# Hybrid DeltaNet and forgetting-attention layer on one core: TensorE multiplies with the values before it computes the scores of a slot

## What is computed

```python
log_f = jax.nn.log_sigmoid(f_logit + f_bias)
cum = jnp.cumsum(jnp.moveaxis(log_f, 2, 1), axis=-1)
for i in range(s // Q_BLOCK):
    lo, hi = i * Q_BLOCK, (i + 1) * Q_BLOCK
    logits = (jnp.einsum('bhqd,bhkd->bhqk', q[:, :, lo:hi], k[:, :, :hi]) * scale
              + cum[:, :, lo:hi, None] - cum[:, :, None, :hi])
    logits = jnp.where(s_pos[None, :] <= t_pos[:, None], logits, -jnp.inf)
    p = jax.nn.softmax(logits, axis=-1)
    outs.append(jnp.einsum('bhqk,bhkd->bhqd', p, v[:, :, :hi]))
```

## Time and profile before

| | us |
|---|---|
| median of 3 runs | 1672.39 |
| lowest, highest run | 1666.14, 1672.8 |
| the profiled execution, its own time | 1669.44 |
| its span, first to last instruction | 1667.3 |
| TensorE busy (matmul) | 1561.4 |
| VectorE, ScalarE, GpSimd busy | 921.2, 692.0, 626.6 |

### The profile page before, as it was taken

One profiled execution on the slowest core, in us unless ns is written; L12 is line 12 of the kernel. 1 busy time (PEld: TensorE's weight loads), 2 busy tenths in 40 slices (PEclk: granted clock), 3 DMA queues, 4 the chain that ended last, 5 costly groups with the idle time before them and its releaser, 6 DMA issues. The chain is left out here.

```text
span 1667.3 us, 22226 instructions
## 1 busy us (share of the span) xinstructions
PE 1561.4 (94%) x7916; PEld 1232.5 (74%) x7916; DVE 921.2 (55%) x1427; ACT 692.0 (42%) x1307; POOL 626.6 (38%) x547
## 2 busy tenths in 40 slices
PE   7999999999999999999749999999999999959998
PEld 5888888888878888888626776766676777637886
DVE  7355545555277668001136676666677766434765
ACT  0346363636211111311005766766676776720100
POOL 1212121202211111110115887867787887901111
PEclk9999999999999999999859999999999999979999
DMA  6134343434753333224491646553555542162642
GB/s 243 46 122 139 89 146 95 135 102 126 115 124 124 122 114 106 68 74 107 124 234 30 166 114 168 140 140 89 140 144 158 154 110 80 38 219 89 202 139 88
DMA packets 191009, 206.81 MB, mean 124 GB/s; under 512 B 50836, under 2 KB 134548, under 8 KB 187860
## 3 DMA queue, kind: packets, MB, share of 16 engines
q1 hardware_dynamic: 189588, 200.35, 42.9%
q10 hardware_dynamic: 1312, 5.05, 0.8%
HBM read 129.98 MB, written 75.30 MB: 123 GB/s over the span
## 5 line engine op out<-in xcount | busy, mean ns | idle before, releaser
L1437 POOL TENSOR_TENSOR m_p_lo<-m_p,m_p_hi 128x512 fp32r<-128x512 f32 (+1 forms) x320 | 373.6, 1189 | 85.8 <-ACT m_p_hi L1394 82.2
L507 PE MATMUL bank<-x_hi,w_hi 128*128 128x512 f32 x992 | 394.5, 398 | 4.1 <-DVEq L801 4.1
L507 PE MATMUL bank<-x_hi,w_lo 128*128 128x512 f32 x992 | 387.8, 391 | 0.0
L507 PE MATMUL bank<-x_lo,w_hi 128*128 128x512 f32 x992 | 387.2, 390 | 0.0
L532 POOL TENSOR_TENSOR w_lo<-w_raw,w_hi 128x512 fp32r<-128x512 f32 x66 | 97.6, 1500 | 498.0 <-ACT w_hi L588 498.0
L1392 ACT ACTIVATE m_p<-m_st,m_fcol 128x512 f32<-128x512 f32 (+1 forms) x320 | 204.1, 638 | 186.3 <-PE m_st L1268 93.1
L1500 DVE TENSOR_REDUCE m_maxima<-m_aux 128x1 f32<-128x512 f32 (+2 forms) x320 | 195.3, 619 | 140.3 <-PE m_aux L1238 90.3
L507 PEld LDWEIGHTS bank<-x_hi,w_hi 128*128 128x128 f32 x992 | 186.8, 188 | 40.9 <-issue 4.5
L507 PEld LDWEIGHTS bank<-x_hi,w_lo 128*128 128x128 f32 x992 | 186.6, 188 | 39.8
L507 PEld LDWEIGHTS bank<-x_lo,w_hi 128*128 128x128 f32 x992 | 186.9, 188 | 36.5
L1394 ACT ACTIVATE m_p_hi<-m_st,m_fcol 128x512 fp32r<-128x512 f32 (+1 forms) x320 | 202.4, 633 | 0.0
(11 more groups left out here) (193 smaller groups left out, 2369.2 us busy)
## 6 DMA issues: line engine op xcount, KB each, us to landing
w_raw<-in_w SPq DMA_DIRECT2D x31, 512.0 KB, 3.9
dram_feat<-ring SPq DMA_DIRECT2D x48, 256.0 KB, 3.3
arena<-dram_gates SPq DMA_DIRECT2D x32, 256.0 KB, 5.0
m_K<-dram_k_hi SPq DMA_DIRECT2D x16, 512.0 KB, 8.2
m_Q<-dram_q_hi SPq DMA_DIRECT2D x64, 128.0 KB, 4.4
o_y<-dram_mixT SPq DMA_DIRECT2D x16, 512.0 KB, 6.1
o_x<-in_x SPq DMA_DIRECT2D x16, 512.0 KB, 4.1
out<-o_res SPq DMA_DIRECT2D x15, 512.0 KB, 5.0
```

The lines of the kernel that those rows point to most:

```text
L507: mm = pe.matmul(banks[bank_of(s)][:], w[:, i % 2, k * P:(k + 1) * P], x[:, k, b * BLOCK:(b + 1) * BLOCK], start=(k == 0 and n == 0), stop ...
L1437: pool.tensor_tensor(p_lo[(s - 1) % PL][:, off:], p[(s - 1) % PL][:, off:], p_hi[(s - 1) % PH][:, off:].bitcast(F32), ALU.subtract).then_i ...
```

## The change

In TensorE's loop the two parts of a slot change places: first the products with the values of three units back, then the scores of the slot's unit. Nothing else is edited.

```diff
                 for s in range(END_SLOT + 1):
+                    if 0 <= s - LAG < N_UNITS:
+                        values(s - LAG)
                     if s < N_UNITS:
                         scores(s)
-                    if 0 <= s - LAG < N_UNITS:
-                        values(s - LAG)
                     for item in AUX_AT.get(s, ()):
                         do_aux(item)
```

## The result

The changed kernel takes 1677.53 us in the median of 17 runs (1671.31 to 1685.53), the kernel before 1672.39 in 17 runs beside it. The medians lie 5.1 us apart. The ratio, which compares runs taken side by side, is 1.0035 with a 95% interval of 1.002 to 1.005: 5.9 us more, with 3.3 to 8.4 in the interval. It lies within the 0.5% that I called no change, and in the range, but on the other side of zero than the -1 to -2.4 us forecast, and clear of noise.

What follows compares the result with a forecast made beforehand. TensorE was taken to bound the kernel. Holds +6.3, weight loads -5.3 and earlier values -2.0 summed to -1.0 us, giving 1668.4 from the profiled execution or 1671.4 from the median; forecast 1670 us, range 1657 to 1685.

Steps and rivals of the forecast that it cites:

- What bounds the kernel: Whole program: TensorE busy over 94% of 1667.3 us, so a microsecond it loses or saves is the program's, unless waits absorb it.
- The first term: Value products waiting for GpSimd's low parts in the attention stage: margins overdrawn in 32 units, 17 bursts, +6.3 us.
- the rule: Low-part margins: 0.47 us less, proportionally for narrower units, and 0.70 us less what GpSimd's queue takes up.
- The rival in which the queue takes up nothing: Values' wait for the low part: TensorE held up to 1.17 us in 22 bursts, net +12.8 us; chance 0.23 with milder kind.
- the 25 that I had named as its sign: Attention stage: waits for low parts above 25 us would speak for the slower outcome.
- The second term: TensorE's weight loads after short products: 9.3 us gained at slot starts, 3.9 lost before maxima, together 5.3 us gained.
- My sign for it: After chain items, first and second score products would stand 0.23 us apart, not 0.32.
- The third term: A group's last values end 0.47 us earlier for VectorE's denominator copy, cutting TensorE's waits for maxima by 2 us.
- The late load of queries: SP's queue: the maximum's queries, held behind a chunk load with TensorE idle 3.67 us until 1143.07, would stay late.

Runs made afterwards that it cites:

- the run with the scores between: Changed order, but scores placed after the two high-part value products and before the low-part product, against the kernel before: 1672.31 us, ratio 0.9997.

## Why the prediction was wrong

**What bounds the kernel: right.** TensorE's lost time in the attention stage came through to the whole: 6.5 us there in one execution, 5.9 by the ratio. What failed is the price of the two gains that I set against it.

**The first term, holds at the low part: right in place, a little low in size.** I had listed 32 units in 17 bursts. Of the 21 listed ahead of the last burst, 17 show a late last value product in the change; five that were not listed do so, too, and in the last burst it is units 309, 311, 312, 318 and 319. The extra hold in a unit is near what the rule gives, 0.44 us at unit 18, where 0.46 was the most that it gave a burst outside the last slots. The sum is +8.1 us for 6.3. That the queue on GpSimd takes up the later scores is borne out by the run with the scores between: 0.47 us later, and no loss. The rival in which the queue takes up nothing, +18.1 us of holds, did not happen, though the loader's 23.8 us stands not far below the 25 that I had named as its sign.

**The second term, loads of weights: the step that failed first.** I took 5.3 us of gain, of which 5.0 (96 x 0.052) came from the ends of 128-wide chain items, with the note that "for the chain ends this is the nearest row, not the row itself". These are such places, with a chain item and the two products behind it, scores before and values after:

```profile
1070.61 0.60 PE L1336 MATMUL m_chain<-m_ident,m_on 128*128 128x128 f32 x4
...
1070.97 0.48 PE L1267 MATMUL m_st<-m_Q,m_K 128*128 128x512 f32 x1
...
1071.29 0.40 PE L1268 MATMUL m_st<-m_Q,m_K 66*128 66x512 f32 x1
```

```profile
1079.84 0.60 PE L1336 MATMUL m_chain<-m_ident,m_on 128*128 128x128 f32 x4
...
1080.19 0.47 PE L1283 MATMUL m_pv<-m_p_hi,m_v_hi 128*65 128x512 f32 x1
1080.51 0.39 PE L1284 MATMUL m_pv<-m_p_hi,m_v_lo 128*64 128x512 f32 x1
```

The second product stands 0.32 us behind the first in both, where I had expected 0.26 with values. From the last chain product to the second product behind it, both 512 wide, it is 0.343 us in the median, for 0.350 with scores: 0.007 saved, not 0.052. Chain products start 0.112 us apart and 512-wide products 0.23; together that is the 0.343, so next to nothing was there to be saved, and 96 x 0.045 = 4.3 us of the gain did not exist. My sign for it, score products 0.23 us apart instead of 0.32, did come, and meant nothing: the 0.32 had moved to the value products. The mask products of maxima and the 64-wide items gave what was expected where a 512-wide product follows (0.302 us for 0.356, 0.431 for 0.488), and the loss behind the mask products of the scores came too (0.358 for 0.304):

```profile
1094.64 0.23 PE L1270 MATMUL m_st<-m_over_k,m_ident_b 128*128 128x128 bf16 x1
1094.68 0.48 PE L1238 MATMUL m_aux<-m_K,m_QM 66*128 66x512 f32 x1
1095.00 0.27 PE L1324 MATMUL m_chain<-m_S,m_q 128*128 128x128 f32 x1
```

All told the usual distances fell by 2.7 us in my account (1.4 to 4.6 by other ways to take them), for the 5.3 predicted and the 1.0 that the corrected term leaves. Where the rest comes from is not shown. I had costed all widths alike, and for narrower products the distances are others: the second product of 256-wide scores follows in 0.117 us in the median instead of 0.201, the second value product in 0.150 instead of 0.120.

**The third term, values that end earlier: real, and worth next to nothing. It failed, too.** VectorE's waits before the denominators fell from 13.8 to 7.4 us, but TensorE's waits for maxima hardly followed (19.1 to 19.0 us in the account; by the waits, 7.0 to 5.8 on TensorE and 15.4 to 14.3 on its loader). I had taken 2 us, from a bound and without a row that tied the two waits together.

With what was measured the sum is 8.1 - 2.7 - 0.1 = +5.3 us, and the ratio says +5.9; the 5.3 is as uncertain as its middle term. Against the forecast, the holds are off by 1.8 us, the loads by 2.6 and the earlier values by 1.9, all in one direction. The forecast of -1.0 was the difference of terms each as large as the thing to be told. Two of three were gains, neither of them wholly read from rows of its own, and both came out smaller.

**The other steps.** The loader's waits rose by 12.5 us in 18 places, for 5 to 10 in a dozen. ScalarE's waits for low parts fell from 13.2 to 4.0 us and are not quite gone. GpSimd's idle time for ScalarE stayed near 76 us as said (79.4); in both kernels some 17 us of it are one stop in the first units. The late load of queries stayed, too. That GpSimd would wait more for finished values (2.9 to 9.3 us) I had not named, and the run with more buffers shows no cost of it. The 131 ns that the Trainium skill (TensorE: Matmul & The Clock Gate, Back-to-back issue gap) gives for a wide product in a stream with loads stand against 0.23 us in the profile after as before. One line ahead of the prediction was wrong: the rounded exponential (line 1394) waits for the values of unit s - 4, since p_hi has four buffers, not for those of s - 3. No number hung on it.

## What to carry to other kernels

In a loop that runs several units deep, the order within a slot is a due time. Take every unit's margin at the product that reads it, count how many are thinner than the shift, and expect each burst of them to be paid once; a thin tail of margins costs even where the median is ample. Give the margin back with one more slot of lag before arguing about order, and look at once for the next result of the same engine, since TensorE may only arrive earlier at the next wait: here the holds came back at the row product until that was moved too, and the pair of edits won 0.5 to 0.6% where either alone won nothing or lost. Price a small gain only from the row that shows that very sequence.

## What the runs showed of the hardware

What the width of the weights costs depends on the product ahead, and not by its length alone. From the start of a product to the second start behind it, with 512-wide products following, it is 0.356 us with 128-column weights and 0.302 with 65 behind a bf16 product of 128 columns. It is 0.488 and 0.431 behind 64 x 64 fp32 products, which are spaced at 0.058 us. But behind a 128-column fp32 product, spaced at 0.112 us, it is 0.350 and 0.343, although the loads themselves are listed with 0.19 and 0.14 us, longer than those 0.112. Why they hide there is not shown. Behind 512-wide products it doesn't show: they start 0.23 us apart with either load.

A stop of TensorE for a late load has a second part. After 3.67 us idle the granted clock had dropped to 0.50, the lower level of 1.2 GHz, for the stretch behind it, while it is 1.00, 2.4 GHz, in stretches such as 1000 to 1100 us. The windows view of the kernel before (stretch, its length, busy time of PE, PEld, DVE, ACT and POOL with instructions, granted clock, DMA share, GB/s):

```profile
1143.00:1149.00 6.00, 5.93 (x20) 4.69 (x21) 2.93 (x5) 2.53 (x4) 1.76 (x2) 0.50 0.34 109
1000.00:1100.00 100.00, 96.11 (x562) 68.55 (x560) 67.24 (x127) 70.19 (x133) 79.12 (x71) 1.00 0.57 148
```

Wide products followed there at 0.43 us instead of 0.23 (starts of 1143.63 and 1144.06 for two score products of 512 columns).
